# Two activation buffers at another place modulo 512 bytes: 128 behind the weights' place in place of 192

## The chip, the cores and the metric

The kernel runs on one core of a Trainium2 chip. The metric is the device time of one execution in microseconds (us). The profile is one execution taken by the hardware profiler; its span runs from the first to the last instruction. Engines are named as in the profile: PE is TensorE's matmul, PEld its weight load, DVE is VectorE, ACT ScalarE, POOL GpSimd, SP SyncE.

## The reference, cut to what matters

Two blocks follow each other on 256 tokens of width 1024, all in float32. The first block has a state-space branch, a gating branch, a cross attention with a memory of 256 tokens, and a feed-forward layer. The second has two layers, each on the token stream x and (but for the last layer's tail) on a context stream, with a Fourier branch, a convolution, two attentions, four gates, and a feed-forward layer.

```python
def swiglu(hn, w_gate, w_up, w_down):
    return (jax.nn.silu(hn @ w_gate) * (hn @ w_up)) @ w_down

def first_block(x, mem, ...):
    memn = rms_norm(mem, mem_norm_g)
    n = rms_norm(h, mix_norm_g[i])
    proj = n @ w_in[i]
    ...
    merged = gate_a * (ya @ w_proj_a[i]) + gate_b * (yb @ w_proj_b[i])
    h = h + merged @ w_out[i]
    h = h + memory_cross_attention(rms_norm(h, xattn_norm_g[i]), memn, w_q[i], w_k[i], w_v[i], w_xo[i])
    h = h + swiglu(rms_norm(h, ffn_norm_g[i]), w_gate[i], w_up[i], w_down[i])

def second_block(x, c, ctx, ...):
    for l in range(2):
        px = jnp.split(hx @ w_in[l], SPLIT_IDX, axis=-1)
        pc = jnp.split(hc @ w_in[l], SPLIT_IDX, axis=-1)
        x = x + g_m * mixer_stream(px, lp, cos, sin, ctx_kv, lam, lam_init)
        ...
        x = x + g_f * swiglu_2(modulate(rms_norm_2(x, norm_ffn[l]), sh_f, sc_f), w_ffn1[l], w_ffn3[l], w_ffn2[l])
    return rms_norm_2(x, final_norm)
```

## The kernel before

Every weight matrix is read from DRAM in units of 1 MB, 128 partitions by 2,048 float32. SP issues the loads into the four slots of `raw`, in the order of `schedule()`. ScalarE rounds a unit to float32r into one of four slots of `w_high` (line 369), VectorE subtracts and puts the rest into one of two slots of `w_rest` (line 375). TensorE multiplies in three products, high by high, high by rest, rest by high (`product`, whose matmul is line 774), and adds all of them up in the banks of `L`. A unit is 16 weight tiles of 128 x 128, so 48 matmuls with 256 moving columns each, and in front of each the load of its 128 weight columns. TensorE runs the load for the next matmul while the present one streams.

The moving operand is the normed activation, split in the same way into `n_high` (written by ScalarE, line 1342 and others) and `n_rest` (written by VectorE, line 1738 and others), 8 chunks of 256 columns each; the hidden layer `hid_high` and `hid_rest` in the down products; `b_high` and `b_rest` in the products of the branches. In `rows_linear` the two change roles: a tile of n is loaded as weights and the weights' unit streams. The attention's own products take their operands from `work_r`, `hx_r`, `hc_r` and `qd_r`.

The passes of the second block are called c0, x0, c1 and x1 (stream and layer; c1 computes keys and values alone). Each full pass has the projections, three attention stages that are filled with quarters of gate and projection units (`quarter_unit`), the output product, and a feed-forward layer: `ffn_up` of 22 units that alternate gate and up, `ffn_down` of 11. The order on each engine is written out by hand; the engines wait for each other by semaphores alone.

All tensors stand in on-chip memory in the order in which they are allocated, one behind the other in every partition. `raw` and `w_high` take 32,768 bytes of a partition each, `w_rest` 16,384, n_high and n_rest 8,192 each; a weight tile is 512 bytes of a partition and a chunk of n 1,024, so all weight tiles begin at one place modulo 512, and all chunks of n at one place too. Two pads that nothing reads or writes, `ahead_of_n` and `behind_n`, stand around n_high and n_rest. With the first at 192 bytes, n begins 192 bytes behind the weights' place modulo 512. Adding up the other allocations, `hid_high`, `hid_rest`, `b_high`, `b_rest`, `work`, `work_r`, `m` and `gate` begin 192 bytes behind it as well, and `hx`, `hc`, `hx_r`, `hc_r`, `qd_r` and `kv` at the weights' own place.

Of the kernel before, what the change touches and what calls it, by code (L numbers as in the profile page):

```python
# [27 lines left out]
P = 128  # L28
# [120 lines left out]
def build(nc, t, out, consts):  # L149
    ctx = ExitStack()  # L150
    with ctx:
        def sb(name, shape, dt=F32):
            return ctx.enter_context(nc.sbuf_tensor(name, shape, dt))
# [8 lines left out]
        with over:  # L162
            s5z = over.enter_context(nc.sbuf_tensor("s5z", [P, 4096], F32))
        w_rest = sb("w_rest", [P, REST, UNIT], F32R)
        ahead_of_n = sb("ahead_of_n", [P, 48])
        n_high = sb("n_high", [P, DC, T], F32R)
        n_rest = sb("n_rest", [P, DC, T], F32R)
        behind_n = sb("behind_n", [P, 208])
        over = ExitStack()
        with over:  # L170
            hx = over.enter_context(nc.sbuf_tensor("hx", [P, DC, T], F32))
# [2245 lines left out]
```

## Time and profile before

| | us |
|---|---|
| median of three runs | 2605.57 |
| lowest and highest of the three | 2596.77, 2606.48 |
| the profiled execution's own time | 2614.58 |
| its span, first to last instruction | 2612.8 |

| engine | busy us | share of the span |
|---|---|---|
| TensorE, matmuls | 2291.9 | 88% |
| TensorE, weight loads | 2115.4 | 81% |
| VectorE | 1711.6 | 66% |
| ScalarE | 1034.0 | 40% |
| GpSimd | 269.0 | 10% |

The mean granted TensorE clock is 0.933 of full speed. Matmuls are pipelined: one is shown busy from its start to its modelled end, and the next begins long before that end. So a mean duration says little about the rate, and the distance between starts says it all; where a window is filled with matmuls, their count in it gives that distance.

### The profile page before, as it was taken

The page shows a single profiled execution, that of the slowest core. Times are in us where ns is not written, and L with a number is a line of the kernel's source. Part 1 is how long each engine was busy: PE and PEld are TensorE (multiplying, and loading weights), DVE is VectorE, ACT ScalarE, POOL GpSimd, SP SyncE. Part 2 cuts the span into 40 slices and gives each one's busy share as a digit, 9 for nine tenths or more (in the row PEclk, how much of TensorE's full clock was granted, in tenths as well). Part 3 has the DMA queues.
Part 4 walks back from the last instruction along what each step waited for, and adds up shares of the span by engine and source line. Part 5 has one row for each costly group of instructions (what it writes and reads, how often), then busy time and mean ns, then how long its engine had stood idle before and what let it go on. Part 6 is the DMA issues. An engine that isn't in the chain of part 4 may idle for free.

```text
span 2612.8 us, 42890 instructions
## 1 busy us (share of the span) xinstructions
PE 2291.9 (88%) x17529; PEld 2115.4 (81%) x17529; DVE 1711.6 (66%) x2085; ACT 1034.0 (40%) x1196; POOL 269.0 (10%) x277
## 2 busy tenths in 40 slices
PE   4766678988999988989999968989998986998998
PEld 4731177987999987889999957889998985888998
DVE  5689942456555897756548877756546887775554
ACT  4301142344434445534334426534334434544332
POOL 2857400001000001000000011000000002100000
PEclk8977797999999999999999979999999997999999
DMA  5358752442655543344556512245555542333552
GB/s 159 113 210 323 264 170 81 158 133 82 199 193 179 162 146 97 114 161 155 183 177 186 162 65 81 97 146 161 193 177 155 160 129 65 97 97 115 192 186 87
DMA packets 289715, 392.52 MB, mean 150 GB/s; under 512 B 7911, under 2 KB 256030, under 8 KB 282911
## 3 DMA queue, kind: packets, MB, share of 16 engines
q1 hardware_dynamic: 285868, 383.59, 45.0%
q10 hardware_dynamic: 3282, 5.74, 0.7%
q8 instruction: 109, 1.79, 0.3%
q0 software_dynamic: 416, 1.08, 0.3%
q14 instruction: 40, 0.32, 0.0%
HBM read 387.14 MB, written 3.15 MB: 149 GB/s over the span
## 4 chain that ended last, share of the span: by engine, by line
PE 69%; DVE 18%; ACT 3%; issue 3%; POOL 1%; DVEq 0%; ACTq 0%
PE L L774 58%; PE M L774 4%; DVE w_rest L375 3%; PE M L912 1%; DVE m L2023 1%; DVE gate L2023 1%; DVE work L2218 1%; DVE m L1729 1%; DVE n_rest L1738 1%; PE M L1160 1%; POOL work_r L752 1%; DVE work L2323 1%; DVE s5z L2018 1%; DVE work L2195 1%; DVE rstd L1726 1%
## 5 line engine op out<-in xcount | busy, mean ns | idle before, releaser
L774 PE MATMUL L<-n_high,w_high 128*128 128x256 f32 x3584 | 1031.0, 288 | 52.9 <-DVE n_rest L1738 18.1
L774 PE MATMUL L<-n_rest,w_high 128*128 128x256 f32 x3584 | 1013.6, 283 | 0.0
L774 PE MATMUL L<-n_high,w_rest 128*128 128x256 f32 x3584 | 1013.2, 283 | 0.0
L375 DVE TENSOR_TENSOR w_rest<-raw,w_high 128x2048 fp32r<-128x2048 f32 x311 | 714.2, 2298 | 290.3 <-PE L L774 285.3
L369 ACT ACTIVATE w_high<-raw 128x2048 fp32r<-128x2048 f32 x311 | 594.8, 1914 | 430.5 <-PE L L774 392.8
L774 PEld LDWEIGHTS L<-n_high,w_high 128*128 128x128 f32 x3584 | 691.2, 193 | 83.8 <-issue 54.8
L774 PEld LDWEIGHTS L<-n_high,w_rest 128*128 128x128 f32 x3584 | 692.3, 193 | 0.0
L774 PEld LDWEIGHTS L<-n_rest,w_high 128*128 128x128 f32 x3584 | 691.0, 193 | 0.4
L774 PE MATMUL L<-hid_high,w_high 128*128 (+1 forms) x704 | 196.6, 279 | 6.1 <-DVE hid_rest L2120 6.1
L774 PE MATMUL L<-hid_high,w_rest 128*128 (+1 forms) x704 | 195.6, 278 | 0.0
L774 PE MATMUL L<-hid_rest,w_high 128*128 (+1 forms) x704 | 195.5, 278 | 0.0
L2218 DVE SCALAR_TENSOR_TENSOR work<-work,tapc 128x256 f32<-128x256 f32 x360 | 155.9, 506 | 5.9 <-DVE work L2190 1.9
L774 PE MATMUL L<-b_high,w_high 128*128 128x256 f32 x432 | 130.4, 302 | 31.4 <-DVE b_rest L2179 14.2
L774 PEld LDWEIGHTS L<-hid_high,w_high 128*128 128x128 f32 x704 | 132.9, 189 | 7.0 <-DVE hid_rest L2120 7.0
L774 PEld LDWEIGHTS L<-hid_rest,w_high 128*128 128x128 f32 x704 | 133.4, 189 | 0.1
L774 PEld LDWEIGHTS L<-hid_high,w_rest 128*128 128x128 f32 x704 | 132.9, 189 | 0.0
L752 POOL TENSOR_TENSOR hc_r<-kv,hc_r 128x512 fp32r<-128x512 f32 (+1 forms) x16 | 20.8, 1305 | 1055.4 <-ACT hc_r L1385 1055.4
L2116 DVE TENSOR_TENSOR gate<-gate,L 128x512 f32<-128x512 f32 x44 | 30.3, 688 | 147.4 <-PE L L774 147.4
L774 PE MATMUL L<-b_rest,w_high 128*128 128x256 f32 x432 | 126.0, 292 | 0.0
L774 PE MATMUL L<-b_high,w_rest 128*128 128x256 f32 x432 | 125.7, 291 | 0.0
L774 PEld LDWEIGHTS L<-b_high,w_high 128*128 128x128 f32 x432 | 87.8, 203 | 37.8 <-DVE b_rest L2179 14.8
L1391 ACT ACTIVATE work<-M,soft 128x512 f32<-128x512 f32 (+1 forms) x104 | 62.6, 602 | 138.9 <-DVE soft L1843 106.4
(369 smaller groups left out, 2981.6 us busy)
## 6 DMA issues: line engine op xcount, KB each, us to landing
raw<-in_w_in SPq DMA_DIRECT2D x116, 1024.0 KB, 5.5
raw<-in_w_ffn SPq DMA_DIRECT2D x99, 1024.0 KB, 5.2
raw<-in_w_ada SPq DMA_DIRECT2D x48, 1024.0 KB, 8.0
raw<-in_w_out SPq DMA_DIRECT2D x16, 1024.0 KB, 5.0
raw<-in_w_gate SPq DMA_DIRECT2D x11, 1024.0 KB, 5.3
raw<-in_w_up SPq DMA_DIRECT2D x11, 1024.0 KB, 5.2
raw<-in_w_down SPq DMA_DIRECT2D x11, 1024.0 KB, 4.9
raw<-in_w_four SPq DMA_DIRECT2D x6, 1024.0 KB, 5.1
```

What stands on the lines that cost most here:

```text
L369: nc.scalar.activation(w_high[:, u.first % 4, :], raw[:, u.first % 4, :], ACT.Copy).then_inc(high_ready, 1)
L375: nc.vector.tensor_tensor(w_rest[:, u.first % 2, :], raw[:, u.first % 4, :], w_high[:, u.first % 4, :].bitcast(F32), ALU.subtract).then_in ...
L752: nc.gpsimd.tensor_tensor(rest, src, high.bitcast(F32), ALU.subtract).then_inc(op_rest, 1)
L774: ins = mm(dst, a, b, start=first and i == 0, stop=last and i == 2, skip_group_check=skip)
L912: ins = mm(M[:, 0, 0:T], ones[:, :], m[:, c, :], start=c == 0, stop=c == DC - 1)
L1160: ins = mm(M[:, c // 2, c % 2 * T:(c % 2 + 1) * T], y1[:, c, a, k * P:(k + 1) * P], dft256[:, k, a, :], start=i == 0, stop=i == 3)
L1391: A(exps[i % 3][:, 0:nk], score_bank[x["g"] % 2][:, 0:nk], ACT.Exp, bias=soft[:, x["g"] % 4, 0:1], accum_out=soft[:, x["g"] % 4, 2:3]).the ...
L1726: link(V.reciprocal(rstd[:, :], rstd[:, :]))
L1729: V.scalar_tensor_tensor((m if dst is None else dst)[:, c, :], h[:, c, :], gain(c), rstd[:, :], ALU.mult, ALU.mult).then_inc(scaled, 1)
L2023: V.tensor_tensor_scan(dst[:, r, :], s5c[:, 0, tile + r:tile + r + 1].to_broadcast((P, T)), src[:, r, :], 0.0, ALU.mult, ALU.add).then_inc ...
L2116: V.tensor_tensor(hh, sg, L[:, k2, :], ALU.mult).then_inc(dve_step, 1)
L2218: V.scalar_tensor_tensor(acc[:, c, :], conv_in[:, c, bass.ds(k, T)], tapc[:, l, bass.ds(4 * k + c, 1)], acc[:, c, :], ALU.mult, ALU.add).t ...
```

## The change

The first pad shrinks from 48 to 32 float32, the second grows from 208 to 224. n_high and n_rest move down by 64 bytes, to 128 bytes behind the weights' place modulo 512; every tensor behind the pads stays. The instructions of every engine and their order are the same.

```diff
--- before.py
+++ after.py
@@ -162,10 +162,10 @@
         with over:
             s5z = over.enter_context(nc.sbuf_tensor("s5z", [P, 4096], F32))
         w_rest = sb("w_rest", [P, REST, UNIT], F32R)
-        ahead_of_n = sb("ahead_of_n", [P, 48])
+        ahead_of_n = sb("ahead_of_n", [P, 32])
         n_high = sb("n_high", [P, DC, T], F32R)
         n_rest = sb("n_rest", [P, DC, T], F32R)
-        behind_n = sb("behind_n", [P, 208])
+        behind_n = sb("behind_n", [P, 224])
         over = ExitStack()
         with over:
             hx = over.enter_context(nc.sbuf_tensor("hx", [P, DC, T], F32))
```

## Rows read from the trace of the kernel before

**Rows 1.** The page: span, busy us with share and instructions, the chain's lines.

```profile
span 2612.8 us, 42890 instructions
...
PE 2291.9 (88%) x17529; PEld 2115.4 (81%) x17529; DVE 1711.6 (66%) x2085; ACT 1034.0 (40%) x1196; POOL 269.0 (10%) x277
...
PE L L774 58%; PE M L774 4%; DVE w_rest L375 3%; PE M L912 1%; DVE m L2023 1%; DVE gate L2023 1%; DVE work L2218 1%; DVE m L1729 1%; DVE n_rest L1738 1%; PE M L1160 1%; POOL work_r L752 1%; DVE work L2323 1%; DVE s5z L2018 1%; DVE work L219
```

**Rows 2.** Groups of instructions: count | busy us, mean ns | idle before, its releaser.

```profile
L375 DVE TENSOR_TENSOR w_rest<-raw,w_high 128x2048 fp32r<-128x2048 f32 x311 | 714.2, 2298 | 290.3 <-PE L L774 285.3
L369 ACT ACTIVATE w_high<-raw 128x2048 fp32r<-128x2048 f32 x311 | 594.8, 1914 | 430.5 <-PE L L774 392.8
```

**Rows 3.** Windows in the four ffn_up stretches: busy us and instructions by engine.

```profile
core 0: us, PE busy (x) PEld busy (x) DVE busy (x) ACT busy (x) POOL busy (x), PEclk, DMA share, GB/s
660.00:760.00 100.00, 100.00 (x884) 100.00 (x884) 58.13 (x46) 39.13 (x29) 0.00 (x0) 1.00 0.59 189
1200.00:1300.00 100.00, 100.00 (x851) 100.00 (x850) 56.46 (x45) 38.25 (x27) 0.00 (x0) 1.00 0.58 182
1790.00:1890.00 100.00, 100.00 (x885) 100.00 (x884) 57.07 (x45) 38.98 (x27) 0.00 (x0) 1.00 0.62 196
2420.00:2520.00 100.00, 100.00 (x852) 100.00 (x851) 57.09 (x45) 38.87 (x27) 0.00 (x0) 1.00 0.59 187
```

**Rows 4.** Timeline, TensorE, ffn_up of x0: start us, duration us, instruction.

```profile
1787.88 0.28 PE L774 MATMUL L<-n_rest,w_high 128*128 128x256 f32 x1
...
1788.90 0.28 PE L774 MATMUL L<-n_rest,w_high 128*128 128x256 f32 x1
```

**Rows 5.** Timeline, TensorE, ffn_up of c0, nine steps again.

```profile
1199.91 0.28 PE L774 MATMUL L<-n_rest,w_high 128*128 128x256 f32 x1
...
1200.97 0.28 PE L774 MATMUL L<-n_rest,w_high 128*128 128x256 f32 x1
```

**Rows 6.** Timeline, TensorE, values of two heads of x0's differential attention, full clock.

```profile
1567.53 1.60 PE L774 MATMUL M<-work_r 128*128 128x256 f32 x12
...
1586.27 1.60 PE L774 MATMUL M<-work_r 128*128 128x256 f32 x12
```

**Rows 7.** The same kind of product at half clock: timeline, window, group.

```profile
583.57 2.34 PE L774 MATMUL M<-work_r 128*128 128x256 f32 x10
...
583.60:585.60 2.00, 2.00 (x11) 2.00 (x10) 0.42 (x1) 0.48 (x2) 1.74 (x2) 0.50 0.00 0
...
L774 PE MATMUL M<-work_r 128*128 128x256 f32 x12 | 2.9, 427 | 4.1 <-POOL work_r L752 4.1
```

**Rows 8.** Windows in the looped part of the four ffn_down stretches, first one.

```profile
772.00:812.00 40.00, 40.00 (x355) 40.00 (x354) 17.18 (x9) 14.19 (x8) 0.00 (x0) 1.00 0.62 202
```

**Rows 9.** Groups of matmuls by line 774, one of the three products each.

```profile
L774 PE MATMUL L<-n_high,w_high 128*128 128x256 f32 x3584 | 1031.0, 288 | 52.9 <-DVE n_rest L1738 18.1
L774 PE MATMUL L<-hid_high,w_high 128*128 (+1 forms) x704 | 196.6, 279 | 6.1 <-DVE hid_rest L2120 6.1
L774 PE MATMUL L<-b_high,w_high 128*128 128x256 f32 x432 | 130.4, 302 | 31.4 <-DVE b_rest L2179 14.2
...
L774 PE MATMUL L<-w_high,n_high 128*128 128x256 f32 x256 | 73.0, 285 | 6.3 <-DVE w_rest L375 6.3
```

**Rows 10.** Timeline, TensorE, rows_linear of c1 and of x1, n loaded as weights.

```profile
1993.95 0.28 PE L774 MATMUL L<-w_rest,n_high 128*128 128x256 f32 x1
...
1994.97 0.28 PE L774 MATMUL L<-w_rest,n_high 128*128 128x256 f32 x1
...
2095.80 0.28 PE L774 MATMUL L<-w_rest,n_high 128*128 128x256 f32 x1
...
2096.86 0.28 PE L774 MATMUL L<-w_rest,n_high 128*128 128x256 f32 x1
```

**Rows 11.** Groups of ScalarE and VectorE that write n in the second block.

```profile
L1342 ACT ACTIVATE n_high<-m,mod 128x256 fp32r<-128x256 f32 x56 | 26.5, 505 | 27.3 <-DVE m L1729 27.3
...
L1738 DVE SCALAR_TENSOR_TENSOR n_rest<-m,mod,n_high 128x256 fp32r<-128x256 f32 x56 | 25.3, 480 | 4.7 <-ACT n_high L1342 4.7
```

## Prediction

> **What bounds the kernel now.** I read the page first: TensorE's matmuls are busy 88% of the span, VectorE 66%, and 58% of the chain that ended last is the one line that multiplies weights into L [rows 1]. The idle time of the two engines that split the weights says the same: they wait for TensorE and not the other way round, VectorE 285.3 us and ScalarE 392.8 us [rows 2]. Then four windows of 100 us, one in each gate-and-up stretch of the feed-forward layers (x, c0, x0 and x1, 22 units of 48 matmuls each): TensorE is busy all 100 us, VectorE 56 to 58, ScalarE 38 to 39, DMA at 0.58 to 0.62 [rows 3]. There nothing but the spacing of the matmuls sets the time, and a nanosecond of that spacing goes into the end one to one.
>
> So the quantity to look at is the distance from one matmul's start to the next, not a matmul's own duration (276 or 281 ns, since they overlap). It takes **two values for the same instructions**. The same windows hold 884, 851, 885 and 852 matmuls [rows 3]; take off the two or three that were already under way at the edge, and that is 113.4 and 117.8 ns. The timeline shows it without the edge: nine steps take 1.02 us in one stretch (113.3 ns) [rows 4] and 1.06 us in the other (117.8 ns) [rows 5]. Each stretch keeps its value from its first steps to its end; the code and the places of the tensors are the same in all four. Neither value belongs to the weights' slot or to high or rest: what picks it is something in the moment at which a stretch begins.
>
> **What the places have to do with it.** In every one of these steps TensorE reads 256 columns of the moving operand while it loads the 128 columns of the next weights. Adding up the allocations, the weights lie at one place modulo 512, n_high, n_rest, the hidden layer, b_high and b_rest 192 bytes behind it, work_r with them. A product with both operands in work_r therefore has distance 0 between moving operand and weights, and the trace has some: the twelve matmuls of a head's values in the differential attention take 1.60 us from the first start to the last end; less the last one's 0.28, eleven steps of 120 ns, and the next head's twelve do the same [rows 6]. So distance 0 gives one value, 120, and distance 192 gives 113.3 or 117.8. At half clock (1.2 GHz) the same twelve show 2.34 us over the ten recorded; less 0.43, nine steps of 212 ns, one column in one cycle with nothing on top, at distance 0 too [rows 7]. At 2.4 GHz one column a cycle would be 106.7 ns; the extra 6.7, 11.1 and 13.3 ns are what full speed costs at these distances. They stand in the ratio 3 : 5 : 6, which looks like a wait that is met once, or five times in three, or twice for each matmul. The hidden layer's product, again at 192, holds 355 or 356 matmuls in 40 us in all four layers [rows 8], which is the fast value.
>
> The trace therefore says that distance matters, and has the values for two distances only. The new distance, 128, stands in no row.
>
> **The change, part by part.** It adds and removes no instruction, moves none on any engine, and no wait changes. n_high and n_rest go down by 64 bytes, everything else stays. Four things read or write them.
>
> *The products with n.* 3 x 3,584 with n moving and 3 x 256 with the weights moving and n loaded, 11,520 of the 14,928 matmuls of that line [rows 9]. From the timeline's starts I count, in stretches of twelve or more at full clock, some 5,300 steps of n at 113.3 and some 4,600 at 117.8 (rows of either kind: [rows 4, 5]); the rest begin a stretch, lie in short ones or run at half clock. In the 768 with n loaded the distance is the same with the other sign, and goes from -192 to -128; they show both values too, nine steps in 1.02 us and in 1.06 [rows 10].
>
> Price of a new value, for all of n: all at 113.3 saves 4,600 x 4.4 ns = 20 us. All at 117.8 costs 5,300 x 4.4 ns = 24 us. All at 120, as at distance 0, costs 5,300 x 6.7 + 4,600 x 2.2 ns = 46 us. At 106.7, the value that half clock implies, it saves 5,300 x 6.7 + 4,600 x 11.1 ns = 86 us. These are the bounds on both sides. How much of it reaches the end: 58.0% of 2612.8 is 1515 us of the chain on that line [rows 1], against some 1,760 us that its 14,928 steps take (at about 115.5 ns, plus 0.1 us each for the few at half clock); so 0.86. The missing part lies in the attention stages, where quarter units of gate and projection fill the gaps of the softmax and end early or late for nothing. With it: -17, +20, +39 and -74 us.
>
> *The writers of n.* ScalarE writes n_high in about 0.51 us and VectorE n_rest in 0.48 us a chunk [rows 11], 88 of each, and 24 of double width. A write of one stream at a time; I take nothing. Even 5% would be 112 x 0.03 us = 3 us, most of it under TensorE's first unit.
>
> *hid, b, attention.* Their places stay, so 3,408 matmuls and the two values there stay as they are.
>
> *Loads and splits.* raw, w_high and w_rest stay. If TensorE ran at 106.7 ns a unit would take 5.1 us, and VectorE's split of 2.3 us [rows 2] and the load of 1 MB (0.6 of the DMA engines' time now [rows 3]) would still hide; nothing takes the bound over in the long stretches.
>
> **What I choose.** Likeliest is that 128, like 192, keeps moving operand and weights apart and leaves the same two values, drawn anew at each start: n's steps stay a mixture, and the sum is nil. Two reasons: +192 and -192 (n loaded, weights moving) already show the same pair although they are different distances, so a distance need only be away from 0; and which of the two a stretch gets depends on its beginning, which the change leaves alone. Against the profiled run's 2614.58 us that is 2614.6; the median of the runs shown lies 9 us lower, so 2605. A flip of one long stretch is 1,056 x 4.4 ns = 4.7 us, and the spread of the three runs (9.7 us) is two such flips; I give this case 2595 to 2616.
>
> Beside the sum, a rule. The rows show that the reads of the two operands disturb each other, since spacing depends on their distance. The Trainium skill, "TensorE: Matmul & The Clock Gate", section "Part 2: What happens when you issue a matmul", says that matmul and weight load have separate read ports and that loading the next weights takes nothing from the running matmul. By that rule the change would do nothing and all the rows would have one spacing; the trace disagrees at 113.3, 117.8 and 120 ns. The same page, section "Back-to-back issue gap", puts 256 columns at about 109.2 ns; as an estimate from that figure, all of n there would be 5,300 x 4.1 + 4,600 x 8.6 ns = 61 us less before the 0.86, or 52 with it. No row here shows such a step.
>
> **The rivals.**
>
> *A, it collides as distance 0 does.* If what is shared repeats every 128 bytes or less (two groups of 64 bytes, say), 128 is the same as 0 and every step of n takes 120 ns: +39 us, 2645. For it: 192 and -192 both are 64 modulo 128, so no row tells whether the 512 or the 128 counts. Against it: nothing but that 128 is a long way from 0 in 512. This is the case on the other side, and it decides in the feed-forward stretches: 1,056 steps would take 127 us there in place of 120 or 124.
>
> *B, the slow value becomes the rule.* The new distance is nearer to 0 and widens the set of beginnings that end at 117.8: +20 us, 2626.
>
> *C, the fast value becomes the rule.* Half of n's steps sit at 117.8 today; at another distance that second way may not exist, as at distance 0 there is only one: -17 us, 2588.
>
> *D, below 113.3.* If what is shared repeats every 256 bytes, 128 is as far from 0 as can be, and 192 is not. Halfway between 113.3 and 106.7, at 110, n saves 5,300 x 3.3 + 4,600 x 7.8 ns = 53 us, with 0.86 46 us: 2560. Against it: the fast value is exact to a tenth of a nanosecond in all stretches and looks like a floor.
>
> *E, the change doesn't do what it says.* The pads are plain tensors and everything is allocated in a row, so it does; no chance of its own.
>
> **How the numbers follow.** Mixture as now 0.36 (2605), A 0.19 (2645), B 0.13 (2626), C 0.20 (2588), D 0.12 (2560). No case has a majority. Half a per cent (13 us) is about what a measurement of this kernel can tell from no change. Faster by more than that: D, most of C and a twentieth of the mixture, 0.31. Slower: A, most of B and a twentieth of the mixture, 0.32. Within: 0.37. The range leaves out D and the ends: 2577 (C with 10 us below it) to 2652 (A with nothing hidden).
>
> **What would show it.** In the changed kernel's windows over the four feed-forward stretches: 884 and 851 in 100 us again, in whatever order, is the forecast; 836 in all four is A; 851 in all B; 884 in all C; above 890 D. The same windows over the hidden layer's product must keep 355 or 356 in 40 us, and the twelve of attention 1.60 us, or it isn't the distance that counts. If n's writers or the waits of VectorE changed while spacing did not, my account would be wrong at its root.

## The result, and the profile after

| | before | after |
|---|---|---|
| median, us (4 runs each) | 2603.47 | 2643.97 |
| lowest and highest | 2596.77, 2606.48 | 2640.07, 2648.78 |
| profiled execution, us | 2614.58 | 2648.78 |
| its span, us | 2612.8 | 2647.0 |

The ratio is 1.016, with a 95% interval of 1.0132 to 1.0188: the changed kernel is slower by 1.6%. The forecast was "the same"; rival A's 2645 us is close to the measured time, though its mechanism is only half of what the traces show.

The page of the changed kernel, its lines that answer to [rows 1] (span; busy us by engine; lines of the chain):

```profile
span 2647.0 us, 42890 instructions
...
PE 2331.4 (88%) x17529; PEld 2154.2 (81%) x17529; DVE 1711.0 (65%) x2085; ACT 1034.1 (39%) x1196; POOL 268.9 (10%) x277
...
PE L L774 61%; PE M L774 4%; DVE w_rest L375 2%; PE M L912 2%; DVE m L1729 2%; DVE n_rest L1738 1%; DVE m L2023 1%; DVE gate L2023 1%; DVE work L2218 1%; PE M L1160 1%; POOL work_r L752 1%; DVE work L2323 1%; DVE s5z L2018 1%; DVE rstd L172
```

The same number of instructions runs on every engine. VectorE, ScalarE and GpSimd are busy for the same time within a microsecond; TensorE's matmuls for 39.5 us more, and line 774 has gone from 58% to 61% of the chain. Now the windows in the four ffn_up stretches, as in [rows 3], shifted to where these now lie:

```profile
660.00:760.00 100.00, 100.00 (x846) 100.00 (x845) 56.30 (x45) 38.01 (x27) 0.00 (x0) 1.00 0.59 185
1210.00:1310.00 100.00, 100.00 (x845) 100.00 (x845) 54.78 (x45) 36.99 (x26) 0.00 (x0) 1.00 0.58 187
1810.00:1910.00 100.00, 100.00 (x845) 100.00 (x844) 55.32 (x45) 38.51 (x27) 0.00 (x0) 1.00 0.60 189
2450.00:2550.00 100.00, 100.00 (x845) 100.00 (x844) 55.04 (x45) 36.74 (x26) 0.00 (x0) 1.00 0.59 184
```

884, 851, 885 and 852 matmuls have become 845 or 846 in all four. The timeline of TensorE in the third stretch, to be held against [rows 4, 5]: ten steps from the first of these rows to the last, 1.19 us, where 113.3 ns would have made 1.13 and 117.8 ns 1.18.

```profile
1849.91 0.28 PE L774 MATMUL L<-n_rest,w_high 128*128 128x256 f32 x1
...
1850.50 0.28 PE L774 MATMUL L<-n_high,w_high 128*128 128x256 f32 x1
...
1851.10 0.28 PE L774 MATMUL L<-n_high,w_rest 128*128 128x256 f32 x1
```

From the starts, which are recorded to the nanosecond, the mean over a long stretch is 118.67 ns, with a pattern that repeats after five matmuls (593.3 ns). 89% of n's steps in stretches of 30 or more at full clock have this value, the other 11% have 120.0; neither 113.3 nor 117.8 is left. The hidden layer's product, whose place has not moved, is as it was [rows 8]: windows of 40 us in the looped part of ffn_down of x and of x0 (x1's window holds 356; in c0's the product ends 1.1 us before the window does, and up to there its steps are 113.3 ns too),

```profile
785.00:825.00 40.00, 40.00 (x355) 40.00 (x355) 16.54 (x8) 15.31 (x12) 0.00 (x0) 1.00 0.60 206
...
1940.00:1980.00 40.00, 40.00 (x355) 40.00 (x355) 16.05 (x7) 15.53 (x11) 0.00 (x0) 1.00 0.58 190
```

and the writers of n cost what they did [rows 11]:

```profile
L1342 ACT ACTIVATE n_high<-m,mod 128x256 fp32r<-128x256 f32 x56 | 26.5, 505 | 27.3 <-DVE m L1729 27.3
...
L1738 DVE SCALAR_TENSOR_TENSOR n_rest<-m,mod,n_high 128x256 fp32r<-128x256 f32 x56 | 25.2, 478 | 4.8 <-ACT n_high L1342 4.8
```

**Where the 34 us came from.** n's full-clock steps: 10,950 of 115.53 ns on average before, 10,917 of 118.82 after, +32.2 us. Its half-clock steps (213.3 ns): 361 before, 389 after, +6.0. The products with b and with the hidden layer add 1. Line 774 takes 39 us longer, and 34.2 of it reach the end of the span. Read by cause and not by count, the longer spacing is 36 us (10,950 steps of 3.29 ns more), and the 28 steps more at half clock cost what they have over a full-clock step, 28 x 94.5 ns = 2.6 us.

The medians differ by 40.5 us and the traces by 34. The traced execution of the kernel before was a long one, 2614.58 us, with 57% of the steps in n's long stretches at the fast value; its second trace, further down, has 2605.43 us, 72%, and 9 us less on line 774.

### The profile page after: what moved, and what is told of

Read it like the earlier page. It is cut to its first block, busy times and chain, and to the rows that moved or that the text cites. A ratio compares the mean times of both kernels' runs of the same rounds, so it can differ in the third digit from the quotient of the medians.

```text
span 2647.0 us, 42890 instructions
## 1 busy us (share of the span) xinstructions
PE 2331.4 (88%) x17529; PEld 2154.2 (81%) x17529; DVE 1711.0 (65%) x2085; ACT 1034.1 (39%) x1196; POOL 268.9 (10%) x277
## 4 chain that ended last, share of the span: by engine, by line
PE 72%; DVE 19%; ACT 4%; issue 3%; POOL 1%; DVEq 0%; SPq 0%; DMA 0%; ACTq 0%
PE L L774 61%; PE M L774 4%; DVE w_rest L375 2%; PE M L912 2%; DVE m L1729 2%; DVE n_rest L1738 1%; DVE m L2023 1%; DVE gate L2023 1%; DVE work L2218 1%; PE M L1160 1%; POOL work_r L752 1%; DVE work L2323 1%; DVE s5z L2018 1%; DVE rstd L1726 1%; ACT w_high L369 1%
## 5 line engine op out<-in xcount | busy, mean ns | idle before, releaser
L774 PE MATMUL L<-n_high,w_high 128*128 128x256 f32 x3584 | 1044.0, 291 | 48.3 <-DVE n_rest L1738 17.1
L774 PE MATMUL L<-n_rest,w_high 128*128 128x256 f32 x3584 | 1026.5, 286 | 0.0
L774 PE MATMUL L<-n_high,w_rest 128*128 128x256 f32 x3584 | 1026.0, 286 | 0.0
```

The source lines that it names most:

```text
L774: ins = mm(dst, a, b, start=first and i == 0, stop=last and i == 2, skip_group_check=skip)
```

## The experiments

Short name of each kernel in bold. "Fast share" is the share of n's steps at 113.3 ns among those in stretches of 30 or more at full clock, counted from the recorded starts. All but the last two kernels were executed once beside one execution of the kernel before, so what they tell is told by their traces. A single time is a rough one: ten executions of one of these kernels, further down, lie between 2602.61 and 2619.56 us.

### The distance from 0 to 384

Four kernels differ from the one before in the two pads alone, always so that all else stays in place.

```diff
# d0:   [P, 48], [P, 208]  ->  [P, 128], [P, 128]
# d64:                         [P, 16],  [P, 240]
# d256:                        [P, 64],  [P, 192]
# d384:                        [P, 96],  [P, 160]
-        ahead_of_n = sb("ahead_of_n", [P, 48])
+        ahead_of_n = sb("ahead_of_n", [P, 128])
...
-        behind_n = sb("behind_n", [P, 208])
+        behind_n = sb("behind_n", [P, 128])
```

**d0**

> n_high and n_rest at distance 0 from the weights' place modulo 512 (pads of 512 and 512 bytes), all else as before. Theory R (what is shared repeats every 128 bytes or less): 0 and 128 are the same, so n's steps take 118.7 ns as in the changed kernel, about 845 matmuls in 100 us of ffn_up, time near 2644. Theory S (each distance modulo 512 has its own value, 0 the worst): 120 ns as the attention's products with both operands in work_r, 836 in 100 us, time about 10 us over the changed kernel, near 2654.

**d64**

> n at distance 64. Theory R: 64 is the same as 192 modulo 128, so both values of before, 113.3 and 117.8 ns (884 and 851 in 100 us), time near 2604. Theory S: 64 is nearer to 0 than 128 is, so it is no better than 128: 118.7 to 120 ns (845 to 836), time 2644 to 2654.

**d256**

> n at distance 256, the farthest from 0 in 512. Theory R: 256 is the same as 0 and 128 modulo 128: 118.7 ns or more, 845 or fewer in 100 us, time 2644 or more. Theory S: farther from 0 than 192, so at least as good: 113.3 ns or the pair of before (884, or 884 and 851), time 2585 to 2604.

**d384**

> n at distance 384, which is -128. Theory R: as 128, 118.7 ns, 845 in 100 us, time near 2644. Theory S with distance counted on both sides of 0: the same as 128 as well; with distance counted one way only (the weights' stream runs into the moving one from behind): another value than 118.7.

The windows in the first ffn_up stretch of d0, d256 and d384, in this order:

```profile
660.00:760.00 100.00, 100.00 (x836) 100.00 (x835) 56.92 (x45) 38.61 (x27) 0.00 (x0) 1.00 0.58 181
```

```profile
660.00:760.00 100.00, 100.00 (x836) 100.00 (x835) 53.76 (x42) 37.63 (x27) 0.00 (x0) 1.00 0.58 188
```

```profile
660.00:760.00 100.00, 100.00 (x845) 100.00 (x844) 54.59 (x45) 38.68 (x27) 0.00 (x0) 1.00 0.59 189
```

and of d64 the second and third stretch:

```profile
1200.00:1300.00 100.00, 100.00 (x851) 100.00 (x851) 55.27 (x45) 37.48 (x26) 0.00 (x0) 1.00 0.59 188
1797.00:1897.00 100.00, 100.00 (x885) 100.00 (x884) 57.82 (x46) 40.19 (x28) 0.00 (x0) 1.00 0.63 196
```

| distance | n's steps | fast share | time, us | before beside it |
|---|---|---|---|---|
| 0 | 120.0 | 0 | 2646.99 | 2607.81 |
| 64 | 113.3 and 117.8 | 17% | 2627.03 | 2607.81 |
| 128 (the change) | 118.7, some 120.0 | 0 | 2643.97 | 2603.47 |
| 192 (before) | 113.3 and 117.8 | 57% | 2603.47 | |
| 256 | 120.0 | 0 | 2645.63 | 2607.81 |
| 384 | 118.7, some 120.0 | 0 | 2636.93 | 2607.81 |

Neither theory holds as it was put. S (a value for each distance modulo 512, 0 the worst, 256 the best) falls with 256, which is the equal of 0, and with 64, which is nearer to 0 than 128 and far better. R (128 repeats) is right that multiples of 128 are bad and 64 is good, but wrong that 0 and 128 are the same: 836 matmuls in 100 us against 845. What fits all six is the distance **modulo 256**: 0 gives 120.0; 64 and 192 the pair; 128 gives 118.7 with a little 120.0.

### Does the place count or the distance?

**wmove** moves the weights up by 64 bytes and leaves n, the hidden layer and b where they are.

```diff
+        ahead_of_raw = sb("ahead_of_raw", [P, 16])
         raw = sb("raw", [P, RAW, UNIT])
...
-        ahead_of_n = sb("ahead_of_n", [P, 48])
+        ahead_of_n = sb("ahead_of_n", [P, 32])
```

> The weights (raw, w_high, w_rest) move up by 64 bytes; n, the hidden layer and b stay where they are in the kernel before, so all three now lie 128 bytes behind the weights. If the distance between the two operands counts: n at 118.7 ns (845 matmuls in 100 us of ffn_up), and the hidden layer and b at 118.7 ns as well (338 or 339 in 40 us of ffn_down in place of 355), time about 12 us over the changed kernel, near 2655. If n's own place counts: n, the hidden layer and b keep 113.3 and 117.8 ns, time near 2604.

Two windows in its ffn_up stretches and, of 40 us, two in its ffn_down stretches:

```profile
660.00:760.00 100.00, 100.00 (x845) 100.00 (x845) 55.13 (x42) 37.70 (x27) 0.00 (x0) 1.00 0.59 184
```

```profile
785.00:825.00 40.00, 40.00 (x336) 40.00 (x335) 16.05 (x7) 15.52 (x11) 0.00 (x0) 1.00 0.55 178
1340.00:1380.00 40.00, 40.00 (x340) 40.00 (x339) 16.05 (x7) 15.52 (x11) 0.00 (x0) 1.00 0.55 185
```

n at its old place has 118.7 ns (120.0 in 9% of the steps of its long stretches), and no stretch has 113.3 or 117.8. The hidden layer and b, which no kernel moves, had 113.3 or 117.8 ns in their long stretches in every other trace; here they have neither: 340 in 40 us is 118.7 ns, 336 is 120.0 (from the starts: 79% and 21% of the hidden layer's steps; b's mean is 119.4). The distance between the two operands decides, not the place of either, and it does so for n, the hidden layer and b alike.

### Is each matmul priced by its own pair?

**rest128** and **rest64** leave n_high at 192 and put n_rest alone at 128 or 64 (pads between the two of 448 and 384 bytes, taken from the one behind).

```diff
         n_high = sb("n_high", [P, DC, T], F32R)
+        between_n = sb("between_n", [P, 112])
         n_rest = sb("n_rest", [P, DC, T], F32R)
-        behind_n = sb("behind_n", [P, 208])
+        behind_n = sb("behind_n", [P, 96])
```

> n_high stays at distance 192, n_rest alone goes to 128. Of three matmuls in a row n_rest streams in one, while w_rest is loaded. If each matmul's price depends on its own pair alone, a step is a third of the way from 113.3 or 117.8 to 118.7 ns: 115.1 to 118.1 on average (868 to 846 in 100 us). If the pattern locks over three matmuls as a whole, one of the known values 117.8 or 118.7, or a new one, in every stretch.

> n_high at distance 192, n_rest at 64 (with 128 for n_rest, every stretch had 118.6 to 118.9 ns). If a pair only has to keep off multiples of 128, this gives 113.3 and 117.8 ns as 192 alone does, time 2600 to 2630. If n_high and n_rest have to lie at the same distance for the fast value to lock, no 113.3 ns: 117.8 or more throughout, time over 2620.

One window of each in an ffn_up stretch, rest128 and then rest64:

```profile
1810.00:1910.00 100.00, 100.00 (x844) 100.00 (x844) 55.17 (x45) 38.89 (x27) 0.00 (x0) 1.00 0.59 189
```

```profile
1810.00:1910.00 100.00, 100.00 (x852) 100.00 (x851) 55.01 (x45) 36.96 (x27) 0.00 (x0) 1.00 0.59 187
```

With one pair in three at 128, all stretches with n moving have 118.7 to 118.9 ns, not a third of the way. So the price belongs to the sequence as a whole and is no mean over its pairs. With that pair at 64, all of them have 117.8 and none 113.3. That the fast value needs all three pairs at one distance is not shown by this: with all three pairs at 64 only 17% of n's steps are fast in d64, and 3 and 8% in the later runs at that residue, so one pair at 64 may simply bring 64's odds. And where n is loaded as weights, rest64 has its pairs at two distances as well and yet 113.3 ns in 55% of the 733 steps, 118.9 in the others (rest128 has 115.6 there); this was not followed up. The times were 2640.35 us (before beside it 2613.89) and 2645.65 (2606.08). The second is some 20 us more than a spacing of 117.8 ns cost at 64; some 55 half-clock steps of n more than in d64 are 5 us of that, and the rest stays open.

### Between the multiples of 64

**d160** and **d224**: pads of 40 and 216, and of 56 and 200 float32.

```diff
-        ahead_of_n = sb("ahead_of_n", [P, 48])
+        ahead_of_n = sb("ahead_of_n", [P, 40])
...
-        behind_n = sb("behind_n", [P, 208])
+        behind_n = sb("behind_n", [P, 216])
```

> n at distance 160, between 128 (118.7 ns) and 192 (113.3 or 117.8). If what is shared comes in pieces of 64 bytes aligned to 64, a distance that is no multiple of 64 mixes two neighbours: between 113.3 and 118.7, about 850 to 865 in 100 us. If only the distance modulo 256 in smooth form counts, the same. If a start off 64 costs extra, over 118.7 ns (under 845).

> n at distance 224, between 192 (113.3 or 117.8) and 256 (120 ns). Pieces of 64 bytes: between 113.3 and 120, 836 to 884 in 100 us. A start off 64 that costs extra: over 120 ns (under 836). If odd multiples of 32 were free of the clash, under 113.3 ns (over 884).

At 160 n's long stretches have 117.3 ns (40%) or 118.7 (56%) and in the rest 120.0, at 224 they all have 118.3, between the neighbours 192 and 256. With n loaded as weights the distance has the other sign, so it is 96 and 32 modulo 256, and the steps are 120.0 and 116.7 ns: 96 is as bad as 0, and 32 lies under the 117.8 that is usual at 64. So a distance between two tested ones can't be read off its neighbours. Times 2640.66 and 2635.16 us (before beside them 2613.89). Neither has 113.3 anywhere: of the two places tried between 128 and 256 none beats 192. Nothing finer than 32 bytes was tried.

### Modulo 256, and who draws the fast value

**d448** and **d320** carry on the row of the pads (112 and 144, 80 and 176 float32); **again** is the kernel before, traced a second time.

> n at distance 448, which is 192 modulo 256 and -64. Theory P (the value depends on the distance modulo 256; 0 gives 120, 128 gives 118.7 or 120, 64 and 192 the pair): only 113.3 and 117.8 ns in n's long stretches (884 or 851 in 100 us), time 2600 to 2630. Theory 512 (the runs at 0, 256, 128 and 384 agree by chance): any other value, 118.7 or more, time over 2635.

> n at distance 320, which is 64 modulo 256. Theory P: only 113.3 and 117.8 ns. If 64 and 192 differ in how often a beginning ends at the slow value (at 64, 7 of 8 of n's steps had it, at 192 under half), then mostly 117.8 here, time near 2627 as at 64; if that was chance, any share of the two, 2600 to 2630.

> The kernel before once more, for a second trace of it. If what picks a stretch's value is the moment of its beginning, n's stretches are shared out otherwise than in the first trace (fast, slow, fast, slow in the four ffn_up), both values only, and the time moves with the share, 4.4 ns for every step that changes. If the code picks it, fast, slow, fast, slow again.

One window in the first ffn_up stretch of d448 and of d320, in this order:

```profile
650.00:750.00 100.00, 100.00 (x884) 100.00 (x884) 57.08 (x45) 39.73 (x28) 0.00 (x0) 1.00 0.62 199
```

```profile
660.00:760.00 100.00, 100.00 (x851) 100.00 (x851) 56.49 (x45) 38.90 (x27) 0.00 (x0) 1.00 0.60 189
```

The four ffn_up windows of the second trace of the kernel before; [rows 3] had 884, 851, 885, 852:

```profile
660.00:760.00 100.00, 100.00 (x885) 100.00 (x884) 57.08 (x45) 38.97 (x27) 0.00 (x0) 1.00 0.60 194
1200.00:1300.00 100.00, 100.00 (x851) 100.00 (x850) 56.50 (x45) 38.86 (x27) 0.00 (x0) 1.00 0.59 189
1790.00:1890.00 100.00, 100.00 (x885) 100.00 (x884) 59.13 (x47) 38.99 (x28) 0.00 (x0) 1.00 0.60 189
2420.00:2520.00 100.00, 100.00 (x885) 100.00 (x884) 58.04 (x47) 39.54 (x29) 0.00 (x0) 1.00 0.60 189
```

The fourth stretch has changed sides with nothing changed in the program, so what draws lies outside it: the moment, as far as this tells (the two traces may be of different chips). At 448 and 320 there are both values again and no other, so the period of 256 holds for the four pairs of distances tried. But the odds aren't even. Fast share at 192: 57% and 72%; at 448: 69%; at 64: 17%; at 320: 3%. The 768 matmuls with n loaded, whose distance has the other sign, have the odds the other way round: 13% fast in all four traces at 192 and 448 (for them 64), 36 to 42% in the three at 64 and 320 (for them 192). Times: 2606.20 us at 448, 2605.43 for the kernel before, 2639.92 at 320 (before beside them 2606.08).

To know whether that is a property of the distance, 448 and 64 were timed in rounds, as **t448** and **t64** (same kernels).

> n at distance 448, timed. If the share of the two values belongs to the distance modulo 256: as the kernel before, ratio 0.997 to 1.003, and more of n's long stretches at 113.3 than at 117.8 ns. If it is drawn anew in every execution with even chances: the same ratio, so this run is the control for the next one.

> n at distance 64, timed. If the share belongs to the distance (17% of n's steps in long stretches fast at 64 and 3% at 320, against 57, 69 and 73% at 192, 448 and 192 again): about half of the steps change from 113.3 to 117.8 ns, 11,000 x 0.5 x 4.4 ns x 0.85 = 20 us, ratio 1.005 to 1.011. If it is chance: ratio 0.997 to 1.003.

448: 2610.64 us median against 2604.96, ratio 1.0009 with 0.9991 to 1.0027; fast share 68%. 64: 2624.24 us, ratio 1.0078 with 1.0042 to 1.0113; fast share 8%. All four ffn_up stretches of t64 are slow, three of four of t448 fast; one window of each:

```profile
1800.00:1900.00 100.00, 100.00 (x851) 100.00 (x851) 57.07 (x45) 38.91 (x27) 0.00 (x0) 1.00 0.58 185
```

```profile
1800.00:1900.00 100.00, 100.00 (x885) 100.00 (x884) 58.30 (x46) 40.28 (x29) 0.00 (x0) 1.00 0.61 191
```

All five executions of t64, 2620.26 to 2640.80 us, are longer than all ten of t448 and all fourteen of the kernel before, of which the longest took 2619.56. So 64 and 192 have the same two values and differ in how often a stretch ends at the slow one, and for n that belongs to the distance. It is not the only thing that shifts the odds. The hidden layer's product stands at 192 in all these kernels; its fast share is 87% in the trace of d448 and 41% in that of t448, which is the same kernel. Its window in ffn_down of x, in t448, has 342 matmuls, which is 117.8 ns, where [rows 8] had 355:

```profile
772.00:812.00 40.00, 40.00 (x342) 40.00 (x341) 16.95 (x8) 13.45 (x7) 0.00 (x0) 1.00 0.58 186
```

No kernel of the series is faster than the one before.

## Why the prediction was wrong, point by point

**The bound and the quantity** were right. TensorE bounds the kernel, spacing is what changed, and no other engine changed: VectorE's busy time differs by 0.6 us of 1711.

**The step that failed** is the choice: "a distance need only be away from 0". It rested on 192 and -192 having the same pair. Modulo 256 these two are 192 and 64, the two residues that have the pair, so they said nothing about 128, which turned out to have 118.7 and 120.0 ns. One row of a third residue was needed, and the prediction had none. The trace did hold a sign that the two are not equal: with n moving 57% of the steps in long stretches are fast, with n loaded 13%; the prediction read both only as "both values". The second reason, that the beginning of a stretch draws the value "which the change leaves alone", was right for a given distance (the second trace of the kernel before shows it) and no argument for another: distances have their own sets of values, and 64 has even the same set with other odds.

**Rival A** had the sign and, at 2645 against 2643.97, the time. Its mechanism was half right. It took 128 for the same as 0, with 120 ns; the steps have 118.7, and the period is 256, not 128. That the times agree so closely is luck. Priced was 46 us at full weight, 39 at the end; in the traces the longer spacing is 36 us and the extra steps at half clock, which no step of the sum had, 2.6, and 34 reach the end. Only the medians differ by 40.5 us, and between the traces it was 34, as the traced execution of the kernel before was a long one. Rival B's value (every step at 117.8) is nearly what 64 and 320 show. Its price of 20 us fits the median of t64, 19.3 us over the kernel before; the one execution of 320 was 34 us over, within what t64's five span. D (the fast end at 128, from 256 as the period) had the right period and the wrong end of it.

**The share that reaches the end** was put at 0.86. Measured: 34.2 of 39 us, 0.87. d256 and d384, at 31 of 42 and 22 of 30 us, are somewhat lower, 0.73 to 0.74, the kernel before traced again at 9.2 of 9.4 us higher. Against the busy time of TensorE on their pages (37.7 and 25.7 us more than before) d256 and d384 come to 0.82 and 0.87. So the share is good to a tenth or so, and 0.87 for 0.86 is closer than the method is.

**What the sum left out** is the clock. The two kernels with 128 modulo 256 have the same steps (118.82 and 118.83 ns on average at full clock) and differ by 12 us of span. The one with the longer span has 389 half-clock steps of n, the other 255; 134 steps of 213.3 in place of 118.8 ns are 12.7 us. A stretch of the profile in which that shows is the cross attention and what follows; windows of the changed kernel and of d384:

```profile
560.00:640.00 80.00, 64.30 (x465) 62.08 (x465) 36.99 (x57) 35.63 (x57) 15.15 (x12) 0.87 0.29 93
```

```profile
560.00:640.00 80.00, 63.80 (x462) 61.46 (x461) 34.22 (x57) 33.68 (x57) 15.24 (x12) 0.91 0.32 104
```

The granted clock is 0.87 of full speed in the one and 0.91 in the other (the two levels are 1.2 and 2.4 GHz). What shifted it here was not tried.

**The sign for the hidden layer** (355 or 356 in 40 us, "or it isn't the distance that counts") came true in the changed kernel, but it was not a safe one: t448 has 342 there with the distance unchanged. Only a value outside the pair, as in wmove, speaks of the distance.

**The range** was 2577 to 2652 and held the time. Its top came from the bound "all of n at 120", a row of the trace at distance 0; that bound was the best part of the working. **The chances** gave slower 0.32, less than same, on the wrong choice above.

**The rule of the Trainium skill** that was weighed ("TensorE: Matmul & The Clock Gate", "Part 2: What happens when you issue a matmul", that loading the next weights takes nothing from the running matmul) would have given no change. The runs disagree: wmove moves the weights alone by 64 bytes, and the hidden layer's products go from 355 in 40 us to 340 and 336; the 336 (120.0 ns) stands in no kernel with the old distance.

## What to carry to other kernels

Where float32r matmuls of 256 columns follow each other at full clock, each with a weight load before it, compute the distance in bytes between moving operand and weights modulo 256: 192 was best here (113.3 ns, or 117.8 by the moment), 64 had mostly 117.8, 128 had 118.7 (120.0 in a tenth) and 0 had 120.0. Read it from the count of matmuls in a full window, not from mean durations, and test the residue in an experiment before arguing from it: two distances that look different can be one residue. Don't leave one operand of a sequence behind: one of three at 128 took the whole sequence to 118.7 ns or more. And look at two traces of the same kernel before giving a difference of a few microseconds to an edit.

## What the runs showed of the hardware

- The values at 0, 64, 128 and 192 are simple multiples of one time, 6.667 ns: 17 of them are 113.3, 53 for three matmuls 117.8, 89 for five 118.7, 18 are 120.0. The starts of the fast steps, taken modulo 6.667 ns, stay within about a nanosecond of one phase over the whole span of the kernel before, but for a steady drift of 1.6 parts in a million. Stretches that are far apart share that phase, so they seem to keep step with something that ticks through the whole execution; what ticks is not shown.
- At half clock the distance costs nothing that can be seen: n's steps have 213.3 ns for 256 columns, within half a nanosecond on average, in d0 as in the kernel before ([rows 7] has distance 0 too).
- No stretch of n in any of the thirteen kernels has a step under 113.3 ns on average; half of 213.3 would be 106.7.
- Why the period is 256, why 128 is milder than 0, why 96 is as bad as 0, and why 64 draws the slow value more often than 192 stays open. So does the mechanism: that TensorE's two reads disturb each other is argued from the part that their distance plays, and no trace shows what they share.
